# A three-layer forward pass: the opening and the sums of squares of a norm rearranged

## The chip, the cores and the metric

One core of a Trainium2 chip runs the whole program. The metric is the device time of one execution in microseconds; the kernel before takes 2764.75 us, the median of three runs (2763.87 to 2766.82).

## What is computed

Three transformer-like blocks follow one another on a sequence of 512 tokens of width 1024 (528 with 16 extra tokens in the first block). Each begins with an RMS norm and a wide projection, goes through its own mixing (attention of several kinds, a recurrence, a gated memory), and ends with an output projection, a residual addition, another norm and a gated feed-forward part whose result is added to the residual. What matters here is the norm and the projection behind it:

```python
def _rmsnorm(a, gain):
    af = a.astype(jnp.float32)
    af = af * lax.rsqrt(jnp.mean(af * af, axis=-1, keepdims=True) + EPS)
    return (af * gain.astype(jnp.float32)).astype(a.dtype)
...
    z = u @ w_up
```

Everything is in float32.

## The kernel before

**Layout and units.** The residual stream `h` lies transposed: 8 tiles (chunks) of 128 features by the tokens. A weight unit is 1024 inputs by 128 outputs, 8 chunks of 128x128, and is loaded by SyncE's queue (SP) with one transfer of 512 KB into a ring of four buffers (`load_unit`, L355). To keep float32 accuracy, each operand is split into a high part in the fp32r format and a low part, the rest. A chunk of a unit is three matmuls: high weights with high inputs, high weights with low inputs, low weights with high inputs. ScalarE makes the high weights (`hi`, L363), VectorE the low ones (`lo`, L369), two units ahead of TensorE. The same is done to the inputs: `Inputs` (L665 high on ScalarE, L673 and L675 low on VectorE), or `Normed` (products L710, high L695, low L700), which multiplies by the root first.

**Lines.** A `Line` is a matrix product of n units, a unit per output tile (L594). `Added` is the line that adds each finished tile to the residual (L847, L849 on VectorE); `Glu` is the feed-forward's first half (gates scaled on GpSimd, L904; Silu on ScalarE, L891). `down` is the feed-forward's second half, three `Added` lines in a row of 8, 8 and 6 chunks.

**Order.** Every stage gives each engine's program as a generator that yields a planned time, counted in units, ahead of its instructions; `weave` merges the generators of all stages by these times into one fixed queue per engine. The time only sets the order: an instruction whose wait isn't fulfilled holds up all that stands behind it on its engine. A `Line` yields its chunk k of unit u at `at + u + k/8` on TensorE, its high weights at the end of a unit on ScalarE.

**The sums (`Sums`, L717).** While an `Added` line runs, its finished tiles are squared on ScalarE (L741), the squares of tiles 0 to 6 are added up on GpSimd (L756, six additions into `acc`), and TensorE sums over the features with matmuls by a matrix of ones (L766): first `acc`, planned 0.3 units ahead of the end of the line, then the square of the last tile, planned 0.4 units behind it. ScalarE loads the table set that holds Ln and Exp (L295) right ahead of the last square, and makes the root with Ln (L747) and Exp (L748). There are seven such sums. After three of them (near 628, 1006 and 1463 us) the next line starts from the raw tiles, and the root is multiplied in behind its matmuls. After the two that run side by side near 1845 us (`one` and `two`; `SecondRoot` makes the root of `two` at L797 and L798), and after that near 2376 us, the next line's inputs are products with the root. The last one (2749 us) stands ahead of the output (`Final`, L823).

**The opening.** `Prepare` (L2082 on) loads small constants and parameters on SP, the input in four transfers on ScalarE's queue (L2139), squares it (L2149) and sums the squares on TensorE (L2167). `NormedInput` then loads the table set, makes the root (L405, L407), has the first two weight units split, and makes products (L435), high parts (L414) and low parts (L428) chunk by chunk. The first line, `Halved` (L1991), cuts the 528 tokens in two halves of 264 and does all chunks of the first half, then all of the second (L2028).

Of the kernel before, what the change touches and what calls it, by code (L numbers as in the profile page):

```python
# [239 lines left out]
class Core:  # L240
# [151 lines left out]
class NormedInput:  # L392
# [8 lines left out]
    def high(self, act, first=None):  # L401

        core, T = self.core, self.T
        core.exp_ln(act)
# [12 lines left out]
    def low(self, dve, first=None):  # L417
# [3 lines left out]
        def part(k):  # L421
# [295 lines left out]
class Sums(Stage):  # L717


    def __init__(self, core, at, d, tiles, ready, T, bank, tmp, r, names, gains=None, first=None):  # L720
        self.core, self.at, self.d, self.tiles, self.ready, self.T, self.bank, self.r = core, at, d, tiles, ready, T, bank, r
        self.gains, self.first = gains, first
        self.sq, self.acc = core.area(tmp, 2, T), core.area(tmp + 2 * T, T)
        self.squared, self.added, self.summed, self.root = (core.take(n, k) for n, k in zip(names, (NC, NC - 2, 1, 1)))
# [7 lines left out]
    def scalar(self, act):  # L732
        core = self.core
        for k in range(NC):
            yield self.at + (k + 1) * self.d + 0.25
            if k == NC - 1 and self.first is None:
                core.exp_ln(act)
# [5 lines left out]
        yield self.end() + 0.55  # L743
# [6 lines left out]
    def pool(self, pool):  # L750
        for k in range(1, NC - 1):
# [6 lines left out]
    def tensor(self, pe):  # L758
        for n, a in enumerate((self.acc, self.sq[:, (NC - 1) % 2])):
            yield self.end() + (-0.3, 0.4)[n]  # L760
            if n == 0:
                pe.wait_ge(self.added.sem, self.added.at(NC - 2))
            else:
                pe.wait_ge(self.squared.sem, self.squared.at(NC))
            for e, (o, w) in enumerate(halves(self.T)):
                last = pe.matmul(self.core.ps[:, self.bank + e, 0:w], self.core.c("ones"), a[:, o:o + w], start=(n == 0), stop=(n == 1))  # L766
# [1224 lines left out]
class Halved(Stage):  # L1991
# [20 lines left out]
    def tensor(self, pe):  # L2012
        core = self.core
        for u in range(self.n):
            s = self.first + u
            wh, wl = core.wh[:, s % 2], core.wl[:, s % 2]
            for e, (o, m) in enumerate(self.cols):
                for k in range(NC):
                    yield self.at + u + (8 * e + k) / 16
                    if k == 0:  # L2020
                        if self.free.at(2 * u + e - 1) > 0:
                            pe.wait_ge(self.free.sem, self.free.at(2 * u + e - 1))
                        if e == 0:
                            pe.wait_ge(core.split_done, s + 1)
                    if self.x and u == 0 and e == 0:
                        self.x.ready(pe)(k)
                    for n, (w, x) in enumerate(((wh, core.xh), (wh, core.xl), (wl, core.xh))):
                        last = pe.matmul(self.place(e), w[:, k, :], x[:, k, o:o + m], start=(k == 0 and n == 0),  # L2028
                                         stop=(k == NC - 1 and n == 2))
                last.then_inc(core.used if e else self.half.sem, 1)  # L2030

    def scalar(self, act):
# [6 lines left out]
        if self.x:  # L2039
            self.x.high(act, first)  # L2040
# [13 lines left out]
    def vector(self, dve):  # L2054
# [36 lines left out]
class Prepare(Stage):  # L2091
# [17 lines left out]

    def sync(self, sp):  # L2110
# [3 lines left out]
        sp.dma_start(core.par[:, 0:NC], d["params"][:, 0:NC]).then_inc(self.small.sem, 16)  # L2114
        yield -0.5
# [19 lines left out]
    def scalar(self, act):  # L2135
        core, T = self.core, self.T
        yield -20
        for i in range(4):
# [1534 lines left out]
```

## Time and profile before

| | |
|---|---|
| median of three runs | 2764.75 us |
| the profiled execution | 2761.72 us |
| its span | 2759.9 us |
| mean granted clock of TensorE | 0.972 |
| TensorE matmuls busy | 2617.1 us |
| VectorE, ScalarE, GpSimd busy | 1517.5, 1039.5, 331.8 us |

The span is the time from the first to the last recorded instruction; the execution's own time has 1.8 us more around it. TensorE (PE) is the busiest engine by far. Its records overlap, since matmuls are pipelined: the distance between two starts is the cost of one, not the length of a record. The granted clock is 1.00 at 2.4 GHz and 0.50 at 1.2 GHz.

### The profile page before, as it was taken

How to read it: one execution, taken by the hardware profiler on the slowest of the kernel's cores; microseconds unless marked ns; L12 is line 12 of the kernel's file. 1: busy time of each engine (PE TensorE's matmuls, PEld its weight loads, DVE VectorE, ACT ScalarE, POOL GpSimd, SP SyncE). 2: the span in 40 equal slices, each digit the busy share in tenths (PEclk: the TensorE clock that was granted, in tenths of full speed). 3: DMA queues.
4: the chain of work that ended last, by engine and by line, in shares of the span. 5: the costliest groups of instructions: out<-in, count | busy, mean ns of one | idle time of the engine just before them, and what ended most of it. 6: DMA issues, size and time to landing. Idle time of an engine off the chain costs nothing.

```text
span 2759.9 us, 35657 instructions
## 1 busy us (share of the span) xinstructions
PE 2617.1 (95%) x14330; PEld 2117.2 (77%) x14330; DVE 1517.5 (55%) x2528; ACT 1039.5 (38%) x1824; POOL 331.8 (12%) x270
## 2 busy tenths in 40 slices
PE   7989999999999999999889999999999999899998
PEld 6778788898998866866657777867766677688886
DVE  3787654455445456477746778454743544433444
ACT  3366454433223252234443223255332433322323
POOL 0043310012222010010012222020000000100001
PEclk8999999999999999998899999999989999999999
DMA  3211112222232331320024664232211122233332
GB/s 124 72 47 55 54 56 67 64 91 84 92 93 91 99 130 46 121 70 1 1 69 146 200 201 154 93 106 84 84 58 50 47 91 86 83 94 97 92 99 69
DMA packets 70850, 239.01 MB, mean 87 GB/s; under 512 B 12212, under 2 KB 13109, under 8 KB 70430
## 3 DMA queue, kind: packets, MB, share of 16 engines
q1 hardware_dynamic: 63054, 208.88, 24.2%
q10 hardware_dynamic: 7632, 27.86, 3.0%
q8 instruction: 114, 1.87, 0.3%
q14 instruction: 50, 0.41, 0.0%
HBM read 234.06 MB, written 2.64 MB: 86 GB/s over the span
## 4 chain that ended last, share of the span: by engine, by line
PE 63%; DVE 10%; ACT 4%; issue 2%; POOL 1%; ACTq 0%; DVEq 0%; POOLq 0%
PE ps L594 53%; DVE wl L369 2%; PE ps L2733 2%; ACT wh L363 1%; PE ps L3410 1%; DVE xl L675 1%; PE ps L1798 1%; PE ps L1782 1%; DVE arena L1061 1%; PE ps L1809 1%; DVE arena L3089 1%; PE ps L3396 1%; PE ps L1647 1%; PE ps L766 1%; DVE xl L673 0%
## 5 line engine op out<-in xcount | busy, mean ns | idle before, releaser
L594 PE MATMUL ps<-xh,wh 128*128 128x512 f32 (+1 forms) x2728 | 1013.6, 386 | 25.4 <-DVE xl L675 7.4
L594 PE MATMUL ps<-xl,wh 128*128 128x512 f32 (+1 forms) x2728 | 993.2, 378 | 0.0
L594 PE MATMUL ps<-xh,wl 128*128 128x512 f32 (+1 forms) x2728 | 989.0, 377 | 0.0
L369 DVE TENSOR_TENSOR wl<-ring,wh 128x1024 fp32r<-128x1024 f32 x374 | 471.5, 1261 | 623.2 <-ACT wh L363 622.6
L363 ACT ACTIVATE wh<-ring 128x1024 fp32r<-128x1024 f32 x374 | 395.2, 1057 | 953.7 <-PE ps L594 851.9
L594 PEld LDWEIGHTS ps<-xh,wh 128*128 128x128 f32 x2728 | 503.1, 190 | 157.6 <-issue 45.0
L594 PEld LDWEIGHTS ps<-xh,wl 128*128 128x128 f32 x2728 | 502.3, 190 | 98.3
L594 PEld LDWEIGHTS ps<-xl,wh 128*128 128x128 f32 x2728 | 501.2, 190 | 98.4 <-issue 6.5
L2028 PE MATMUL ps<-xh,wh 128*128 128x264 f32 (+1 forms) x816 | 259.6, 318 | 9.6 <-DVE xl L428 9.6
L756 POOL TENSOR_TENSOR arena<-arena 128x512 f32<-128x512 f32 (+1 forms) x42 | 71.5, 1708 | 1368.6 <-ACT arena L741 1368.6
L2028 PE MATMUL ps<-xl,wh 128*128 128x264 f32 (+1 forms) x816 | 234.3, 287 | 0.0
L2028 PE MATMUL ps<-xh,wl 128*128 128x264 f32 (+1 forms) x816 | 234.2, 287 | 0.0
L2028 PEld LDWEIGHTS ps<-xh,wh 128*128 128x128 f32 x816 | 156.9, 192 | 37.9 <-issue 20.4
L2028 PEld LDWEIGHTS ps<-xl,wh 128*128 128x128 f32 x816 | 157.7, 193 | 1.0
L2028 PEld LDWEIGHTS ps<-xh,wl 128*128 128x128 f32 x816 | 157.2, 193 | 0.0
L847 DVE TENSOR_TENSOR h<-ps,h 128x512 f32<-128x512 f32 (+1 forms) x64 | 44.3, 691 | 151.2 <-PE ps L594 151.2
L904 POOL TENSOR_TENSOR arena<-arena 128x516 f32<-128x516 f32 (+1 forms) x44 | 81.0, 1840 | 220.1 <-ACT arena L883 220.1
L891 ACT ACTIVATE arena<-arena 128x512 f32<-128x512 f32 x44 | 27.8, 632 | 202.8 <-DVE arena L923 202.8
L849 DVE SCALAR_TENSOR_TENSOR h<-ps,mod,h 128x512 f32<-128x512 f32 x40 | 30.0, 751 | 111.6 <-PE ps L594 111.6
L907 POOL TENSOR_TENSOR arena<-arena 128x512 f32<-128x512 f32 x44 | 58.4, 1327 | 159.3 <-ACT arena L891 159.3
L675 DVE TENSOR_TENSOR xl<-arena,xh 128x512 fp32r<-128x512 f32 (+1 forms) x108 | 72.3, 728 | 7.4 <-ACT xh L665 7.3
L1061 DVE CUSTOM_DVE_ANT_0 arena<-arena 128x1024 f32<-128x1024 f32 x48 | 69.8, 1488 | 0.0
(391 smaller groups left out, 2711.9 us busy)
## 6 DMA issues: line engine op xcount, KB each, us to landing
ring<-in_weights SPq DMA_DIRECT2D x374, 512.0 KB, 3.5
arena<-in_w_ada ACTq DMA_DIRECT2D x48, 512.0 KB, 4.5
arena<-in_cmp_w SPq DMA_DIRECT2D x2, 2048.0 KB
h<-in_x ACTq DMA_DIRECT2D x4, 528.0 KB, 6.2
arena<-strip_scratch SPq DMA_DIRECT2D x8, 264.0 KB, 3.7
out_features<-arena SPq DMA_DIRECT2D x8, 256.0 KB, 2.1
con<-in_consts SPq DMA_DIRECT2D x1, 777.0 KB, 10.9
arena<-in_c ACTq DMA_DIRECT2D x1, 512.0 KB, 3.8
```

The source lines that it names most:

```text
L363: act.activation(flat(self.wh[:, s % 2]), flat(self.ring[:, s % RING]), ACT.Copy).then_inc(self.hi_ready, 1)
L369: dve.tensor_tensor(flat(self.wl[:, s % 2]), flat(self.ring[:, s % RING]), flat(self.wh[:, s % 2]).bitcast(F32), ALU.subtract).then_inc(se ...
L594: last = pe.matmul(self.place(u, e), w[:, k, :], x[:, k, o:o + m], start=(k == 0 and i == 0), stop=(k == self.chunks - 1 and i == 2))
L675: ins = dve.tensor_tensor(xl, a, xh, ALU.subtract)
L756: pool.tensor_tensor(self.acc, self.sq[:, 0] if k == 1 else self.acc, self.sq[:, k % 2], ALU.add).then_inc(self.added.sem, 1)
L847: ins = dve.tensor_tensor(out, self.got(u), out, ALU.add)
L849: ins = dve.scalar_tensor_tensor(out=out, in0=self.got(u), scalar=self.scale[u], in1=out, op0=ALU.mult, op1=ALU.add)
L904: pool.tensor_tensor(g, g, self.r_gate, ALU.mult).then_inc(self.gate_scaled.sem, 1)
L907: pool.tensor_tensor(self.mid[:, j, 2], self.mid[:, j, 2], self.r, ALU.mult).then_inc(self.scaled.sem, 1)
L1061: dve.tensor_tensor_reduce(out=w, in0=w, in1=self.spread, scale=1.0, scalar=0.0, op0=ALU.mult, op1=ALU.add, accum_out=self.parts[:, (n + e ...
L2028: last = pe.matmul(self.place(e), w[:, k, :], x[:, k, o:o + m], start=(k == 0 and n == 0), stop=(k == NC - 1 and n == 2))
L2733: last = pe.matmul(core.ps[:, self.place(n) + e, 0:c], w[:, k, :], x[:, k, o:o + c], start=(k == lo and i == 0), stop=(k == hi - 1 and i = ...
```

## The change

1. In the opening, SP issues two of the four input loads, ahead of the weights, and ScalarE the other two. The table load of `NormedInput.high` is taken out, so that the one that `Prepare` issues at the start serves. The two first weight units are split ahead of the root, with the high part made by a copy on VectorE (`first_hi`). The first unit of the first line goes chunk by chunk through both halves.
2. In all sums, GpSimd adds the squares of tiles 0 to 5 only, and TensorE takes three addends: `acc`, the square of tile 6 and that of tile 7. The table load is planned 0.4 units ahead of the end of the line.
3. Three sums (near 628, 1006 and 1463 us) get `late=True`: all three addends stand 0.65 units into the next line, behind its chunk 5, and Ln and Exp at 0.85.

```diff
+    def first_hi(self, dve, s):
+        dve.wait_ge(self.arrived[s], 16)
+        flat = lambda a: a.rearrange("p c n -> p (c n)")
+        dve.tensor_copy(flat(self.wh[:, s]), flat(self.ring[:, s])).then_inc(self.hi_ready, 1)
...
-    def high(self, act, first=None):
+    def high(self, act):
         core, T = self.core, self.T
-        core.exp_ln(act)
...
-        if first:
-            first(act)
-        else:
-            core.split_first(act, core.split_hi)
...
+        first(dve)
         dve.wait_ge(self.root.sem, self.root.at(1))
...
-            if k == 1:
-                if first:
-                    first(dve)
-                else:
-                    core.split_first(dve, core.split_lo)
...
     def scalar(self, act):
         core = self.core
         for k in range(NC):
+            if k == NC - 1 and self.first is None:
+                yield self.end() - 0.4
+                core.exp_ln(act)
             yield self.at + (k + 1) * self.d + 0.25
-            if k == NC - 1 and self.first is None:
-                core.exp_ln(act)
...
-        yield self.end() + 0.55
+        yield self.end() + (0.85 if self.late else 0.55)
...
-        for k in range(1, NC - 1):
+        for k in range(1, NC - 2):
             yield self.at + (k + 1) * self.d + 0.4
...
-        for n, a in enumerate((self.acc, self.sq[:, (NC - 1) % 2])):
-            yield self.end() + (-0.3, 0.4)[n]
+        for n, a in enumerate((self.acc, self.sq[:, (NC - 2) % 2], self.sq[:, (NC - 1) % 2])):
+            yield self.end() + (0.65 if self.late else (-0.5, 0.05, 0.4)[n])
             if n == 0:
-                pe.wait_ge(self.added.sem, self.added.at(NC - 2))
+                pe.wait_ge(self.added.sem, self.added.at(NC - 3))
             else:
-                pe.wait_ge(self.squared.sem, self.squared.at(NC))
+                pe.wait_ge(self.squared.sem, self.squared.at(NC - 2 + n))
...
-            for e, (o, m) in enumerate(self.cols):
-                for k in range(NC):
-                    yield self.at + u + (8 * e + k) / 16
+            halves_first = [(e, k) for e in range(2) for k in range(NC)]
+            chunks_first = [(e, k) for k in range(NC) for e in range(2)]
+            for i, (e, k) in enumerate(chunks_first if self.x and u == 0 else halves_first):
+                o, m = self.cols[e]
+                yield self.at + u + i / 16
...
             for s in range(self.begin, self.first + 2):
+                if self.x:
+                    core.first_hi(dve, s)
                 core.lo(dve, s)
...
+    def load(self, eng, i):
+        two = slice(2 * i, 2 * i + 2)
+        eng.dma_start(self.core.h[:, two], self.core.dram["x"].rearrange("p (c t) -> p c t", c=NC)[:, two]).then_inc(self.x[i].sem, 16)
...
         sp.dma_start(core.par[:, 0:NC], d["params"][:, 0:NC]).then_inc(self.small.sem, 16)
+        for i in (1, 3):
+            self.load(sp, i)
         yield -0.5
...
-        for i in range(4):
-            act.dma_start(core.h[:, 2 * i:2 * i + 2], self.core.dram["x"].rearrange("p (c t) -> p c t", c=NC)[:, 2 * i:2 * i + 2]).then_inc(
-                self.x[i].sem, 16)
+        for i in (0, 2):
+            self.load(act, i)
         core.exp_ln(act)
```

## Rows read from the trace of the kernel before

**Rows 1.** The page, part 1: busy time, share and instructions of each engine.

```profile
PE 2617.1 (95%) x14330; PEld 2117.2 (77%) x14330; DVE 1517.5 (55%) x2528; ACT 1039.5 (38%) x1824; POOL 331.8 (12%) x270
```

**Rows 2.** Waits of TensorE, whole span: us in total, times, longest.

```profile
PE ps L766 <- ACT arena L741: 14.1, 7, 3.2
...
PE ps L766 <- POOL arena L756: 3.8, 2, 3.0
```

**Rows 3.** Timeline, 0 to 42 us: start, us, what, [idle before <- releaser].

```profile
5.51 1.18 ACT L2149 ACTIVATE arena<-h 128x528 f32<-128x528 f32 x2 [1.17 <-DMA par<-in_params]
...
6.29 9.48 PE L2167 MATMUL ps<-arena,con 128*128 128x264 f32 x32 [6.29 <-ACT arena L2149]
...
15.81 1.28 ACT L295 ACT_TABLE_LOAD   x1 [1.25 <-PE ps L2167]
17.10 0.70 ACT L405 ACTIVATE arena<-ps,con 128x528 f32<-128x528 f32 x1
...
18.59 1.45 DVE L435 SCALAR_TENSOR_TENSOR arena<-h,par,arena 128x528 f32<-128x528 f32 x2 [17.73 <-ACT arena L407]
19.96 2.35 DVE L369 TENSOR_TENSOR wl<-ring,wh 128x1024 fp32r<-128x1024 f32 x2
...
22.23 0.70 DVE L428 TENSOR_TENSOR xl<-arena,xh 128x528 fp32r<-128x528 f32 x1
...
23.77 0.64 ACT L414 ACTIVATE xh<-arena 128x528 fp32r<-128x528 f32 x1 [2.33 <-DVE arena L435]
...
30.76 1.50 DVE L428 TENSOR_TENSOR xl<-arena,xh 128x528 fp32r<-128x528 f32 x2
...
39.60 0.28 PE L2028 MATMUL ps<-xh,wl 128*128 128x264 f32 x1
```

**Rows 4.** Windows of the opening: busy per engine, granted clock, DMA share, GB/s.

```profile
7.00:8.00 1.00, 1.00 (x4) 0.80 (x3) 0.00 (x0) 0.00 (x0) 0.00 (x0) 1.00 1.01 412
...
34.00:36.00 2.00, 2.00 (x11) 2.00 (x10) 0.17 (x2) 0.00 (x0) 0.00 (x0) 0.50 0.00 0
...
37.00:38.00 1.00, 1.00 (x9) 1.00 (x8) 0.00 (x0) 0.00 (x0) 0.00 (x0) 0.89 0.00 0
```

**Rows 5.** Timeline near 1006 us, TensorE and VectorE.

```profile
1003.12 0.40 PE L594 MATMUL ps<-xl,wh 128*128 128x512 f32 x1
1003.35 0.40 PE L594 MATMUL ps<-xh,wl 128*128 128x512 f32 x1
...
1004.84 3.08 DVE L673 SCALAR_TENSOR_TENSOR xl<-h,par,xh 128x512 fp32r<-128x512 f32 x3
...
1006.76 2.08 PE L766 MATMUL ps<-arena,con 128*128 128x512 f32 x2 [3.01 <-POOL arena L756]
...
1016.43 1.71 PE L766 MATMUL ps<-arena,con 128*128 128x512 f32 x2 [2.83 <-ACT arena L741]
...
1022.05 0.69 DVE L991 TENSOR_TENSOR arena<-ps,arena 128x512 f32<-128x512 f32 x1 [6.63 <-PE ps L594]
```

**Rows 6.** Timeline of TensorE near 628 and 1463 us.

```profile
631.37 1.14 PE L766 MATMUL ps<-arena,con 128*128 128x258 f32 x4 [1.78 <-ACT arena L741]
632.16 0.59 PE L594 MATMUL ps<-xh,wh 128*128 128x258 f32 x2
...
1468.33 1.13 PE L766 MATMUL ps<-arena,con 128*128 128x512 f32 x2 [1.89 <-ACT arena L741]
...
1484.43 0.47 PE L594 MATMUL ps<-xh,wh 128*128 128x512 f32 x1 [1.06 <-DVE wl L369]
```

**Rows 7.** Timeline near 1845 us, TensorE and ScalarE.

```profile
1839.96 2.35 PE L766 MATMUL ps<-arena,con 128*128 128x512 f32 x4 [0.81 <-POOL arena L756]
...
1845.50 1.28 ACT L295 ACT_TABLE_LOAD   x1
```

**Rows 8.** Timeline near 2382 us, TensorE, and near 2747 us, ScalarE.

```profile
2382.39 2.07 PE L766 MATMUL ps<-arena,con 128*128 128x512 f32 x2 [3.17 <-ACT arena L741]
...
2747.41 1.28 ACT L295 ACT_TABLE_LOAD   x1 [4.94 <-PE ps L594]
```

More of the change, by code:

```diff
@@ L415, in high, with low @@
                            bias=self.shifts[k] if self.shifts else 0.0).then_inc(self.hi.sem, 1)
-    def low(self, dve, first=None):
+    def low(self, dve, first):
         core, T, out = self.core, self.T, self.out
@@ L717, with __init__ @@
 class Sums(Stage):
-    def __init__(self, core, at, d, tiles, ready, T, bank, tmp, r, names, gains=None, first=None):
+    def __init__(self, core, at, d, tiles, ready, T, bank, tmp, r, names, gains=None, first=None, late=False):
         self.core, self.at, self.d, self.tiles, self.ready, self.T, self.bank, self.r = core, at, d, tiles, ready, T, bank, r
-        self.gains, self.first = gains, first
+        self.gains, self.first, self.late = gains, first, late
         self.sq, self.acc = core.area(tmp, 2, T), core.area(tmp + 2 * T, T)
-        self.squared, self.added, self.summed, self.root = (core.take(n, k) for n, k in zip(names, (NC, NC - 2, 1, 1)))
+        self.squared, self.added, self.summed, self.root = (core.take(n, k) for n, k in zip(names, (NC, NC - 3, 1, 1)))
     def end(self):
@@ L758, in tensor @@
     def tensor(self, pe):
-        for n, a in enumerate((self.acc, self.sq[:, (NC - 1) % 2])):
-            yield self.end() + (-0.3, 0.4)[n]
+        for n, a in enumerate((self.acc, self.sq[:, (NC - 2) % 2], self.sq[:, (NC - 1) % 2])):
+            yield self.end() + (0.65 if self.late else (-0.5, 0.05, 0.4)[n])
             if n == 0:
-                pe.wait_ge(self.added.sem, self.added.at(NC - 2))
+                pe.wait_ge(self.added.sem, self.added.at(NC - 3))
             else:
-                pe.wait_ge(self.squared.sem, self.squared.at(NC))
+                pe.wait_ge(self.squared.sem, self.squared.at(NC - 2 + n))
             for e, (o, w) in enumerate(halves(self.T)):
-                last = pe.matmul(self.core.ps[:, self.bank + e, 0:w], self.core.c("ones"), a[:, o:o + w], start=(n == 0), stop=(n == 1))
+                last = pe.matmul(self.core.ps[:, self.bank + e, 0:w], self.core.c("ones"), a[:, o:o + w], start=(n == 0), stop=(n == 2))
         last.then_inc(self.summed.sem, 1)
@@ L2016, in tensor @@
             wh, wl = core.wh[:, s % 2], core.wl[:, s % 2]
-            for e, (o, m) in enumerate(self.cols):
-                for k in range(NC):
-                    yield self.at + u + (8 * e + k) / 16
[L2020 to L2030, printed above, removed]
+            halves_first = [(e, k) for e in range(2) for k in range(NC)]
[3 more added lines that the diff above has]
+                yield self.at + u + i / 16
+                if k == 0:
+                    if self.free.at(2 * u + e - 1) > 0:
+                        pe.wait_ge(self.free.sem, self.free.at(2 * u + e - 1))
+                    if e == 0:
+                        pe.wait_ge(core.split_done, s + 1)
+                if self.x and u == 0 and e == 0:
+                    self.x.ready(pe)(k)
+                for n, (w, x) in enumerate(((wh, core.xh), (wh, core.xl), (wl, core.xh))):
+                    last = pe.matmul(self.place(e), w[:, k, :], x[:, k, o:o + m], start=(k == 0 and n == 0),
+                                     stop=(k == NC - 1 and n == 2))
+                if k == NC - 1:
+                    last.then_inc(core.used if e else self.half.sem, 1)
     def scalar(self, act):
@@ L2039, in scalar @@
         if self.x:
-            self.x.high(act, first)
+            self.x.high(act)
         else:
@@ L2924, in mixing_end @@
     stages += [inputs, out]
-    sums = Sums(core, NC, 1, h, out.ready, T, 4, sums_tmp, r, names)
+    sums = Sums(core, NC, 1, h, out.ready, T, 4, sums_tmp, r, names, late=True)
     inputs = Inputs(core, h, 2 * NC - 1, T, gain("ffn_norm"), out.ready)
@@ L2930, in mixing_end @@
     stages += some
-    sums = Sums(core, last.at, last.d, late, last.ready, SEQ, 4, sums_tmp, core.area(28984, SEQ), names)
+    sums = Sums(core, last.at, last.d, late, last.ready, SEQ, 4, sums_tmp, core.area(28984, SEQ), names, late=True)
     inputs = Inputs(core, late, at - 1, SEQ, gain("attn_norm_2"), last.ready)
@@ L3552, in mixing_end_2 @@
     out = Added(core, at, WHOLE, (6, 7, 0, 1), inputs, NC, h)
-    sums = Sums(core, at, 1, h, out.ready, T, 4, tmp, r, names)
+    sums = Sums(core, at, 1, h, out.ready, T, 4, tmp, r, names, late=True)
     stages = [inputs, out, sums]
```

## The prediction

> **What bounds the kernel now.** I read the page first: TensorE is busy for 95% of the span [rows 1], so a change can only pay where TensorE waits or runs at half rate. Then the waits of TensorE [rows 2]: the matmuls that sum the squares (L766) waited 14.1 us for ScalarE's squares and 3.8 us for GpSimd's adds, 17.9 us over seven sums. The timeline of the opening [rows 3] and of each seam [rows 5 to 8] then shows what is late. The reader should see two kinds of seam. Where the next line starts from the raw tiles (near 628, 1006 and 1463 us) the sums only block TensorE's own queue. Where the next stage needs the root itself (near 1845, 2382 and 2749 us) they lie on the path.
>
> The profiled execution took 2761.72 us, of which 2759.9 are its span; the median is 2764.75, 3.0 above it. The sum is made against the profiled execution and carried over to the median unchanged.
>
> **The opening.** Today TensorE's last sum ends at 15.77 (6.29 + 9.48), a table load of 1.28 follows, then Ln and Exp, and VectorE starts at 18.59 [rows 3]. The load goes: -1.3. From there to the end of the first low part (22.23 + 0.70 = 22.93) are 4.34 us, because VectorE makes two products and then the two weight splits (19.96, 2.35) first. After the change the splits are ahead of the root; one product (half of 1.45), one high part (0.64), one low part (0.70) and two hand-overs of some 0.08 remain, 2.2: another -2.1.
>
> The splits get two copies on VectorE. No copy of 128x1024 is in the rows; bounds are the subtraction of that size (half of 2.35) above and 0 below, and I take the upper end, the nearest row. Copies and splits then take at most 4.7 us. Their cover is the sums: VectorE can use the root at 17.3. They start when the weights land. On SP two input loads now pass the weights; all input (four loads of 528 KB, 2.16 MB) and one unit (128x1024 floats, 0.52 MB) at the 412 GB/s of [rows 4] are 6.5 us after the first bytes near 3 us (an estimate of the start of the loads), so unit 0 lands near 9.5 and unit 1 near 10.8, and the splits end near 14. Three microseconds of cover are left; past them each microsecond is paid in full. The constants and parameters behind on SP move by about 1.5 us too, and cost nothing: the first one is used after the last low part. The input's new order I price at 0: the squares start when the small parameters are there (5.51 [rows 3]) and then keep the common pace of ScalarE and TensorE, not that of the loads. Bounds: a gain of 1, a loss of 0.5.
>
> The inputs are now 3.4 us earlier. Low parts come every 1.42 us (22.23 to 30.76 in six steps), so the last one ends near 28.9 instead of 32.26 (30.76 + 1.50). Today the second half of the unit (24 matmuls) is still to do then, at half rate until 37 us [rows 4], and the unit ends at 39.88: 7.6 us. With both halves in every chunk, six matmuls stand behind the last low part, at some 0.2 us each (11 in the 2.00 us of 34 to 36), with the hand-over 1.4: -6.2. Six at half rate also just fit between two low parts. The opening's sum is 9.6. The clock is the doubt: it was granted at 0.50 (1.2 GHz) while there were gaps, and rose at 37, some 5 us after the last one. If that repeats, the second unit runs some 3.5 us at half rate and loses 1.7; if the closer work lifts the clock sooner, nothing is lost. I take 0.8: **8.8**, between 7 and 11.
>
> **One addend more.** The last square but one is now added by TensorE. At 631.37 an addend starts and the next line's matmuls follow at 632.16 [rows 6]: 0.79. Above it stands the pair's whole record, 1.13. I take 0.8 a sum. GpSimd has one add less; it was waited for at 1006 and 1840 only.
>
> **Seams where the sums only block.** There they move behind chunk 5 of the next line's first unit.
> Near 628 a wait of 1.78 goes and 0.8 comes: **1.0**, between 0 and 1.8. The table load, now among the high parts, delays the last ones by 1.28, and the last square by less; five chunks hide that.
> Near 1006 both waits (3.01 and 2.83) and the half rate behind each go [rows 5]. From the last matmul before the first wait (ends 1003.75) to the first addition after the next unit (1022.05) are 18.3 us. After the change there are 30 matmuls of 0.23 and three addends of 0.8 in it, 9.3. I add 1.2 for new waits: tile 7 is added behind the low parts on VectorE, so its square comes near 1012.0, some 0.4 after the first two addends, and chunks 4 and 5 wait a little for their low parts. That leaves 7.8; I take **7.5**, between 4 and 8.5.
> Near 1463 a wait of 1.89 goes and 0.8 comes. But root, Silu table and first high part follow on ScalarE at the time of before, since six chunks and three addends take as long as four chunks, the wait and one addend. The fourth unit's weights then come no earlier, and the wait of 1.06 at 1484.43 [rows 6] becomes 2: **0**, between a loss of 0.5 and a gain of 1.
>
> **Seams where the root is the path.** Near 1845 [rows 7] the 0.81 wait for GpSimd goes and the load of 1.28 leaves the path; the two roots share ScalarE, and the earlier one clears it for the other: **2.5**, between 1.3 and 3. Near 2382 [rows 8] the load goes, and the last addend, now after a pause of 1 us instead of 3.17, should take 1.0 at the full rate instead of 2.07: **2.3**, or 1.0 if the clock stays down. Near 2749 the last square waits for VectorE's addition (some 0.75, as long as a product) instead of the load of 1.28 [rows 8]: **0.5**, between 0.3 and 0.7.
>
> The load is followed at once by the next instruction: 15.81 + 1.28 = 17.09, and Ln starts at 17.10 [rows 3], so a load off the path is worth 1.28. The Trainium skill (ScalarE: Activation LUTs, "What ACT_TABLE_LOAD costs") puts a drain of 1.38 us beside each load; by it four loads off the path give an estimated 5.5 us more. The rows don't show it.
>
> **Sum:** 8.8 + 1.0 + 7.5 + 0 + 2.5 + 2.3 + 0.5 = 22.6. 2761.72 - 22.6 = 2739.1 for the profiled execution, 2764.75 - 22.6 = **2742** for the median. The bounds together give 13 to 28 us.
>
> **Rivals.**
> 1. *New waits take the place.* With the table load among the high parts and low parts at the pace of 1.03 (3.08 for three [rows 5]), the last square comes some 3 us later than I think, and the sums wait for it where they now stand. For it: they still wait for the last square. Against: six chunks (4 us) stand ahead. The seam at 1006 gives 4, 628 gives 0, the others 3, the opening 7: 14 us, 2751. Chance 0.20.
> 2. *More than forecast.* The clock rises early in the opening, two queues start the squares sooner, and 1463 keeps its microsecond: 29 us, 2736. Chance 0.11.
> 3. *A pause that the records hide at each table load*, of the load's own length: 4 x 1.28 = 5.1 more, 2737. Against: the 0.01 us between load and Ln. Chance 0.02. (This is the drain of the Trainium skill's page above.)
> 4. *It doesn't reach the end.* VectorE, the busiest engine beside TensorE in the first block, swallows the opening's gain, and the new addends (7 x 0.8 = 5.6) most of the others': 2761. Against: nothing in the first block starts before the opening's line. Chance 0.05.
> 5. *Slower.* The opening's line now keeps a short gap in every chunk, at 0.50. If the clock stays there beyond that line, each microsecond at half rate costs half of one. It decides once such stretches grow by 2 x (22.6 + 5.5) = 56 us; at 70 us the kernel takes 2777, 12 more than before. Against: gapless work raised it at 37. Chance 0.03.
>
> At 1006 the records show what a pause does: 3.01 us without work, and the pair behind it takes 2.08. The Trainium skill (TensorE: Matmul & The Clock Gate, "HAM oscillation") says of waits between bursts that the next burst starts throttled each time; by that rule, too, the trace agrees.
>
> **Numbers.** The forecast has 0.59; its own range is 2737 to 2748. To hold 8 in 10 the range takes in the first rival: 2735 to 2753. Differences within 0.2% (5.5 us) can't be told from none. Faster 0.91, same 0.06, slower 0.03.
>
> **What would show it.** In the opening: no table load near 15.8, VectorE's copies done before 14, the first low part near 19.4, the first unit done near 30. At 1006: no wait at L766 above 1 us and no half rate. At 1463: the wait for the low weights grows to 2. Near 2382: Ln starts 2 to 2.5 us sooner after the unit's end. L766 has 48 matmuls instead of 32, and its waits are under 4 us together. A first unit that ends after 33, or waits above 8 us at L766, would make the forecast wrong.

## The result, and the profile after

| | before | changed |
|---|---|---|
| median, five runs each | 2766.82 us (2763.87 to 2767.0) | 2742.64 us (2737.73 to 2749.81) |
| ratio to before | | 0.9922, 95% interval 0.9909 to 0.9934 |
| profiled execution | 2761.72 us | 2737.73 us |
| its span | 2759.9 us | 2735.6 us |
| mean granted clock | 0.972 | 0.978 |

By the ratio the changed kernel is faster by 0.78% (21.6 us); the two medians differ by 24.2 us. The forecast was 2742 us. The two profiled spans differ by 24.3 us. Beside [rows 1], part 1 of the page of the changed kernel:

```profile
PE 2610.8 (95%) x14346; PEld 2114.1 (77%) x14346; DVE 1514.5 (55%) x2530; ACT 1036.0 (38%) x1821; POOL 320.1 (12%) x263
```

TensorE has 16 matmuls more (48 for the sums instead of 32), ScalarE three instructions fewer (one is the table load, two are the opening's high splits) and GpSimd seven. The waits of TensorE over the whole span (us in total, times, longest), to be read against [rows 2]; the line of the sums is L765 now:

```profile
PE ps L591 <- DVE wl L375: 8.2, 10, 2.4
...
PE ps L765 <- ACT arena L740: 1.6, 2, 0.9
```

The 17.9 us at the sums are 1.6 us, and none is for GpSimd. The timeline of the changed kernel's opening, beside [rows 3]:

```profile
1.66 1.28 ACT L295 ACT_TABLE_LOAD   x1 [1.66 <-PEq L3674]
...
4.83 1.18 ACT L2158 ACTIVATE arena<-h 128x528 f32<-128x528 f32 x2 [1.89 <-DMA par<-in_params]
...
9.93 0.69 DVE L369 CAST wh<-ring 128x1024 fp32r<-128x1024 f32 x1 [9.06 <-DMA ring<-in_weights]
...
12.52 1.23 DVE L375 TENSOR_TENSOR wl<-ring,wh 128x1024 fp32r<-128x1024 f32 x1
...
15.23 0.70 ACT L410 ACTIVATE arena<-ps,con 128x528 f32<-128x528 f32 x1 [1.29 <-PE ps L2176]
...
16.64 1.45 DVE L437 SCALAR_TENSOR_TENSOR arena<-h,par,arena 128x528 f32<-128x528 f32 x2 [2.89 <-ACT arena L412]
...
18.11 0.71 DVE L429 TENSOR_TENSOR xl<-arena,xh 128x528 fp32r<-128x528 f32 x1
...
26.66 1.50 DVE L429 TENSOR_TENSOR xl<-arena,xh 128x528 fp32r<-128x528 f32 x2
...
29.44 1.06 ACT L363 ACTIVATE wh<-ring 128x1024 fp32r<-128x1024 f32 x1
```

The first weights land at 9.93; copies and splits are done at 13.75, ahead of the root. Ln follows the last sum with no load between. The last row is the high part of the next weight unit, which needs the end of the first unit; the same instruction in the kernel before:

```profile
38.17 1.06 ACT L363 ACTIVATE wh<-ring 128x1024 fp32r<-128x1024 f32 x1 [4.32 <-PE ps L2028]
```

So the opening gave 38.17 - 29.44 = 8.7 us. Near 1006 us, beside [rows 5], TensorE and VectorE of the changed kernel:

```profile
996.24 2.07 DVE L670 SCALAR_TENSOR_TENSOR xl<-h,par,xh 128x512 fp32r<-128x512 f32 x3
...
1000.00 0.50 PE L591 MATMUL ps<-xh,wh 128*128 128x512 f32 x1 [0.58 <-DVE xl L670]
...
1001.48 2.90 PE L765 MATMUL ps<-arena,con 128*128 128x512 f32 x6
1003.82 0.79 PE L591 MATMUL ps<-xh,wh 128*128 128x512 f32 x1
...
1005.88 0.69 DVE L990 TENSOR_TENSOR arena<-ps,arena 128x512 f32<-128x512 f32 x1 [2.22 <-PE ps L591]
```

All six matmuls of the three addends run in one piece, 2.34 us from their start to that of the line's next matmul, 0.78 an addend; one wait of 0.58 stands in place of 3.01 and 2.83. Three low parts in a row take 2.07 us where they took 3.08 [rows 5]. That isn't 1.03 each: taken apart, two of the three took 0.74 and the middle one 1.75. The kernel before:

```profile
1005.50 1.75 DVE L673 SCALAR_TENSOR_TENSOR xl<-h,par,xh 128x512 fp32r<-128x512 f32 x1
```

```profile
1005.17 1.53 POOL L756 TENSOR_TENSOR arena<-arena 128x512 f32<-128x512 f32 x1 [4.83 <-ACT arena L741]
```

GpSimd's addition of a square ended at 1006.70, and the long low part 0.55 us behind it. It is the same near 622.81 and 1459.81 us; in the changed kernel no addition stands beside a low part. Near 628 and 1463 us, beside [rows 6]:

```profile
622.58 2.78 PE L765 MATMUL ps<-arena,con 128*128 128x258 f32 x12
...
1472.35 0.47 PE L591 MATMUL ps<-xh,wh 128*128 128x512 f32 x1 [2.44 <-DVE wl L375]
```

The wait at 628 is gone. At 1463 the wait for the fourth unit's low weights grew from 1.06 to 2.44. Near 1845 and 2382 us, beside [rows 7, 8], TensorE and ScalarE:

```profile
1828.18 1.28 ACT L295 ACT_TABLE_LOAD   x1
...
1831.60 3.98 PE L765 MATMUL ps<-arena,con 128*128 128x512 f32 x8
...
2359.52 1.12 PE L765 MATMUL ps<-arena,con 128*128 128x512 f32 x2 [0.89 <-ACT arena L740]
2360.68 0.69 ACT L746 ACTIVATE arena<-ps,con 128x512 f32<-128x512 f32 x1 [1.22 <-PE ps L765]
```

The load stands 3.4 us ahead of the sums, and the last addend takes 1.12 instead of 2.07.

**Where the 24.3 us are.** I lined up the same instruction in both traces (ScalarE's high weights, one a unit) and read how much sooner it starts in the changed kernel: 8.7 us behind the opening, 7.2 ahead of the seam at 628, 8.6 behind it, 16.2 behind 1006, 11.7 ahead of 1463 and 10.5 behind it, 13.6 behind 1845, 12.1 at 2021, 21.5 at 2053, 23.8 behind 2382. The seams are the forecast's; the rest lies between them, and one piece, 9.4 us from 2021 to 2053, is as large as the opening. There the memory gates of the third block are computed, in code that the change doesn't touch. The window from 2000 to 2060 us (length, busy time of PE, PEld, DVE, ACT and POOL with counts, granted clock, DMA share, GB/s), in the kernel before and in the changed one:

```profile
2000.00:2060.00 60.00, 54.06 (x161) 34.29 (x160) 22.82 (x37) 23.07 (x35) 0.00 (x0) 0.77 0.17 53
```

```profile
2000.00:2060.00 60.00, 56.46 (x210) 38.54 (x211) 22.57 (x36) 21.75 (x32) 0.00 (x0) 0.94 0.20 62
```

At a clock of 0.77, 28 of 60 us are at the half rate (60 x 0.23 x 2); at 0.94 it is 7.

### The profile page after: what moved, and what is told of

The parts are those of the page before. It is cut to its first block, busy times and chain, and to the rows that moved or that the text cites. A ratio compares the mean times of both kernels' runs of the same rounds, so it can differ in the third digit from the quotient of the medians.

```text
span 2735.6 us, 35675 instructions
## 1 busy us (share of the span) xinstructions
PE 2610.8 (95%) x14346; PEld 2114.1 (77%) x14346; DVE 1514.5 (55%) x2530; ACT 1036.0 (38%) x1821; POOL 320.1 (12%) x263
## 3 DMA queue, kind: packets, MB, share of 16 engines
q1 hardware_dynamic: 63342, 209.96, 24.3%
## 4 chain that ended last, share of the span: by engine, by line
PE 64%; DVE 10%; ACT 4%; issue 2%; POOL 0%; ACTq 0%; DVEq 0%
PE ps L591 54%; DVE wl L375 2%; PE ps L2742 2%; ACT wh L363 1%; DVE arena L1060 1%; PE ps L3419 1%; DVE xl L672 1%; PE ps L1797 1%; PE ps L1781 1%; PE ps L1808 1%; DVE arena L3098 1%; PE ps L765 1%; PE ps L3405 1%; PE ps L1646 1%; DVE arena L1837 0%
## 5 line engine op out<-in xcount | busy, mean ns | idle before, releaser
L755 POOL TENSOR_TENSOR arena<-arena 128x512 f32<-128x512 f32 (+1 forms) x35 | 60.2, 1726 | 1343.7 <-ACT arena L740 1343.7
```

The source lines that it names most:

```text
L755: pool.tensor_tensor(self.acc, self.sq[:, 0] if k == 1 else self.acc, self.sq[:, k % 2], ALU.add).then_inc(self.added.sem, 1)
```

## The experiments

I held that the change pays at its own seams, and that the 9.4 us are a matter of the clock. The rivals: the gates' gain belongs to the work that was moved, or it is chance of one execution; and single parts of the change are worth other sums than I gave them. Where a table gives "gain at" a time, it is read in the profiles as above, against the profile of before.

**The changed kernel once more**, without an edit, five executions.

> The changed kernel once more, unaltered, to see what differs between executions of one program. Its five times ranged over 12 us where the kernel before had 3. Theory A (fixed savings): span 2735 to 2748, and wherever it is longer than the first profile, the first line, 1006 and 2382 look the same and the time is lost elsewhere. Theory B (the clock by chance): the memory gates near 2013 us run at half rate for 4 us or for 20 us from one execution to the next, worth up to 9 us, and that is the whole spread.

Measured: 2742.94 us (2740.56 to 2744.44), ratio 0.9921 (0.9908 to 0.9934). The gates' gain is there again (9.4 us). But of the opening's 8.4 us at 52 only 0.7 are left at 175 us. The window from 48 to 68 us of this execution:

```profile
48.00:68.00 20.00, 20.00 (x61) 13.11 (x60) 4.86 (x6) 4.51 (x11) 0.00 (x0) 0.57 0.15 50
```

and of the first profile of the same program:

```profile
48.00:68.00 20.00, 20.00 (x97) 13.61 (x96) 7.86 (x10) 6.60 (x16) 0.00 (x0) 1.00 0.23 64
```

Clock 0.57 in the one, 1.00 in the other; 36 matmuls fewer in the same 20 us. TensorE shows no gap in either. Up to 50.13 us the two timelines are the same within 0.13 us, wait by wait. Small attention matmuls over 32 rows (L2286) stand there between those of the line; one pair takes 1.24 us in this execution

```profile
52.15 1.24 PE L2286 MATMUL ps<-arena 32*128 32x264 f32 x2
```

and 0.71 in the first:

```profile
52.68 0.71 PE L2286 MATMUL ps<-arena 32*128 32x264 f32 x2
```

So one program has executions that differ by a stretch of 17 us at the half rate. Over the timed executions, too, the time goes with the mean clock, though they don't tell which stretch it is (clock, us):

```
changed:      .978 2737.73  .973 2749.81  .977 2742.64  .978 2739.04  .973 2747.35
once more:    .975 2744.44  .975 2743.96  .977 2742.94  .977 2742.84  .976 2740.56
```

**The parts apart.** *Opening only*: the kernel before with part 1 of the change.

```diff
-        core.exp_ln(act)
...
+        first(dve)
         dve.wait_ge(self.root.sem, self.root.at(1))
...
+        for i in (1, 3):
+            self.load(sp, i)
...
-                for k in range(NC):
-                    yield self.at + u + (8 * e + k) / 16
+            for i, (e, k) in enumerate(chunks_first if self.x and u == 0 else halves_first):
```

> Only the opening's edits, all sums as before. Theory A: 8.7 us faster than before, as the two profiles differ at the end of the first unit (38.0 against 29.3), 2756 to 2759. Theory B: the shift alone also moves where half-rate stretches fall, above all at the memory gates, so the gain is anywhere from 4 to 18 us and doesn't equal the 8.7 seen at the first unit.

Measured: 2759.92 us (2752.45 to 2767.86, twelve runs), ratio 0.9983 (0.9971 to 0.9995). *Sums only*: the kernel before with parts 2 and 3.

```diff
-        for n, a in enumerate((self.acc, self.sq[:, (NC - 1) % 2])):
+        for n, a in enumerate((self.acc, self.sq[:, (NC - 2) % 2], self.sq[:, (NC - 1) % 2])):
...
+    sums = Sums(core, NC, 1, h, out.ready, T, 4, sums_tmp, r, names, late=True)
```

> Only the edits of the sums, the opening as before. Theory A: from the two profiles 1.2 near 628, 7.6 near 1006, 0 near 1463, 2 to 3 near 1845, 2.4 near 2382, 0.5 at the end: 14 us, 2751 to 2754. Theory B: 14 at these seams, and up to 9 more or 5 less elsewhere, wherever the clock falls differently.

Measured: 2749.95 us (2747.42 to 2753.92), ratio 0.9949 (0.9937 to 0.9961). By medians (before 2765.65, once more 2742.94) the sums are worth 15.7 us, the opening 5.7, both together 22.7. The opening's 8.7 us are there at 38 us in the profile of the opening alone too (8.9), but the half rate at 52 us (clock 0.57 there as well) takes 7.7 of them (8.6 at 52, 0.9 at 175). Its twelve executions spread over 15 us, clocks 0.967 to 0.974.

**The sums not moved** (*not late*): the changed kernel with its three `late=True` taken out.

```diff
-    sums = Sums(core, at, 1, h, out.ready, T, 4, tmp, r, names, late=True)
+    sums = Sums(core, at, 1, h, out.ready, T, 4, tmp, r, names)
```

> The changed kernel with no sum moved into the next line: all at -0.5, 0.05 and 0.4 units. Forecast theory (the move removes the waits near 628, 1006, 1463): waits come back at L765 there, about 1 us at 628, 2 to 3 at 1006 with half rate behind it, and the time is 4 to 7 us longer than the changed kernel. Rival (the earlier table load and the addends on TensorE had done it): no wait above 0.5 us comes back, and the time is the same within 1 us.

Measured: 2753.62 us (2752.22 to 2758.19), ratio 0.9963 (0.995 to 0.9975); 10.7 us more than the changed kernel once more. At 1006 the seam itself still gives 6.2 of the 7.6 us, since two waits have become one of 2.2. But 4.7 us go again between two high parts behind it (those at 1028.58 and 1040.07 us in the kernel before), at a half rate from 1023 to 1033 us of this run. It begins 13 us after the end of that wait. The windows of this run:

```profile
1016.00:1020.00 4.00, 4.00 (x18) 2.93 (x16) 2.28 (x5) 2.41 (x4) 0.00 (x0) 1.00 0.46 131
1020.00:1024.00 4.00, 3.50 (x10) 1.97 (x10) 2.57 (x5) 2.82 (x4) 0.00 (x0) 0.87 0.10 8
1024.00:1028.00 4.00, 4.00 (x7) 1.31 (x5) 0.30 (x1) 0.69 (x1) 0.00 (x0) 0.50 0.33 123
```

That the wait causes it is not shown. The table load alone (below), with waits of 3.0 and 1.3 us here, loses 4.7 us in the same place; the addends alone, with a longer wait (2.7), lose nothing.

At 1463 the sum that was left in place is better, by 2.4 us: a gain across the seam of 1.2 instead of a loss of 1.2. And the gates are back at a clock of 0.74 from 2000 to 2060 us.

**Table load only** and **addends only**, one execution each, on the kernel before. The first plans the table load 0.4 units ahead of the end of the line:

```diff
+            if k == NC - 1 and self.first is None:
+                yield self.end() - 0.4
+                core.exp_ln(act)
             yield self.at + (k + 1) * self.d + 0.25
```

> The kernel before with the table load 0.4 units ahead of the line's end, and nothing else. Forecast theory: the load leaves the path, so against the kernel before the weights' high parts after the seams come 1.3 us sooner at 1845, 1.3 at 2382 and 0.5 at the end; at 628 and 1463 the wait at L766 shrinks by up to 1.3; at 1006 the second wait (2.83) shrinks by up to 1.3 and the first (for GpSimd) stays. If the load costs more on the path than its record (the drain of the Trainium skill's page), it is 2.7 at 1845 and at 2382. Clock theory: outside the seams the profile differs wherever half-rate stretches fall otherwise.

The second has GpSimd add one square less and TensorE three addends at -0.5, 0.05 and 0.4 units:

```diff
-            yield self.end() + (-0.3, 0.4)[n]
+            yield self.end() + (-0.5, 0.05, 0.4)[n]
```

> The kernel before with three addends on TensorE at -0.5, 0.05 and 0.4 units, the table load still ahead of the last square. Forecast theory: the wait for GpSimd near 1004 (3.01) and near 1840 (0.81) is gone; each sum costs TensorE 0.8 more; near 628 and 1463 the next line's first unit ends where it did, because the addend fills the wait for the last square. Near 1006 the last square is still waited for, near 2 us. Rival (TensorE's extra addend costs more than GpSimd's wait): 628, 1463 and 2382 become 0.8 later each.

Measured: 2755.49 and 2758.45 us, before 2767.99. What each gave across a seam, in us:

| seam | table only | addends only | both, not moved | changed |
|---|---|---|---|---|
| 628 | 1.2 | 0.7 | 1.2 | 1.4 |
| 1006 | 3.1 | 5.7 | 6.2 | 7.6 |
| 1463 | 1.2 | 0.8 | 1.2 | -1.2 |
| 1845 | 1.7 | 2.4 | 2.3 | 3.1 |
| 2382 | 1.4 | 0.9 | 2.4 | 2.4 |

The parts overlap, since they clear the same waits. Near 1006 (1000 to 1030 us) the waits of TensorE with the table load alone:

```profile
PE ps L767 <- POOL arena L757: 3.0, 1, 3.0
...
PE ps L767 <- ACT arena L742: 1.3, 1, 1.3
```

and with the addends alone:

```profile
PE ps L766 <- ACT arena L741: 2.7, 1, 2.7
```

Each clears a part of the two waits of [rows 5]: the load more than half of ScalarE's, the addends all of GpSimd's. Where the root is the path (2382), an early load gives 1.4 us, its own length and hardly more.

**The opening's steps.** *Halves first*: the changed kernel with the first unit in its old order.

```diff
-            for i, (e, k) in enumerate(chunks_first if self.x and u == 0 else halves_first):
+            for i, (e, k) in enumerate(halves_first):
```

> The changed kernel with the first unit in the old order, all chunks of one half and then of the other. From the two profiles: the last low part ends at 28.2 as in the changed kernel, and the first unit ends 24 matmuls later than the first half, 3 us at the full rate or 5.3 at half, so near 31.3 or 33.7 instead of 29.2. My forecast had put 6.2 us on this order; the profile of the changed kernel says 4.6 with the clock's share in it. A third outcome, that the gaps in the first half keep the clock at 0.50 as in the kernel before, gives the 33.7.

*Splits behind*: the first weight units are split behind the root again, the high part on ScalarE.

```diff
         act.activation(self.r, self.r, ACT.Exp, scale=-0.5).then_inc(self.root.sem, 1)
+        first(act)
...
-        first(dve)
         dve.wait_ge(self.root.sem, self.root.at(1))
...
+            if k == 1:
+                first(dve)
```

> The changed kernel with the two first weight units split behind the root again, high parts on ScalarE, as before. Forecast theory: the first low part comes 2.1 us later than in the changed kernel, and so does the end of the first unit (31.3 instead of 29.2). Clock theory: TensorE's pause ahead of the first line grows from 3.8 to 5.9 us, so the line starts at 0.50 and is held back by its own matmuls (1.32 per chunk) only where they take over 1.42; then still 2.1. After 50 us both theories leave the profile open: a half-rate stretch of 17 us at 48 to 68 takes 8 us, or doesn't come.

*Delayed*: three more squares of chunk 0, overwritten by the next, stand ahead in `Prepare.scalar` and delay the whole opening.

```diff
+            if k == 0:
+                for _ in range(3):
+                    core.act.do(act, act.activation(self.sq[:, 0], core.h[:, 0], ACT.Square))
```

> The changed kernel with three more squares of the first chunk ahead of the opening's sums, some 2.2 us that nothing covers. Theory A (each span is the sum of its parts): every high part of the weights comes 2.2 us later than in the changed kernel's profiles, from the first to the last. Theory B (half-rate stretches fall by where the work stands in time): 2.2 later at the first unit, then jumps of several us of either sign at 48 to 68, 1236 to 1420 or 2008 to 2050, with half-rate stretches begun or ended there.

Measured, one execution each: 2744.57, 2742.71 and 2741.2 us. The start of the next unit's high part tells the order's price. With halves first:

```profile
27.00 1.50 DVE L429 TENSOR_TENSOR xl<-arena,xh 128x528 fp32r<-128x528 f32 x2
...
34.30 1.06 ACT L363 ACTIVATE wh<-ring 128x1024 fp32r<-128x1024 f32 x1 [4.21 <-PE ps L2029]
```

5.8 us lie between the end of the last low part (28.50) and that start; in the changed kernel 29.44 - 28.16 = 1.3. The order by chunks is worth 4.5 us. The clock's part is in it: with halves first the mean from 0 to 40 us is 0.83, in the changed kernel 0.96. With the splits behind:

```profile
16.15 0.70 ACT L410 ACTIVATE arena<-ps,con 128x528 f32<-128x528 f32 x1 [1.31 <-PE ps L2176]
...
21.28 0.70 DVE L430 TENSOR_TENSOR xl<-arena,xh 128x528 fp32r<-128x528 f32 x1
```

The first low part comes 5.13 us after Ln's start, 2.88 in the changed kernel: 2.2 for the splits. The delayed kernel starts the same high part at 32.40, 3.0 later (2.2 were expected), and is some 3 us behind the changed kernel from there to 2399 us (23.8 against 20.4), with no jump of the clock between.

**What the gates depend on.** In 14 profiles the window from 2000 to 2060 us has one of a few clocks:

| the sum near 1463 | profiles | clock |
|---|---|---|
| moved behind chunk 5 | changed, once more, sums only, halves first, splits behind, delayed, filled | 0.94 in all seven |
| in its old place | before, opening only, not late, table only, addends only, moved twice | 0.77, 0.74, 0.74, 0.89, 0.77, 0.74 |
| old place, gates filled | gates filled | 0.97 |

*Moved twice*: the changed kernel with the sum near 1463 in its old place (the other two stay late), five executions.

```diff
     out = Added(core, at, WHOLE, (6, 7, 0, 1), inputs, NC, h)
-    sums = Sums(core, at, 1, h, out.ready, T, 4, tmp, r, names, late=True)
+    sums = Sums(core, at, 1, h, out.ready, T, 4, tmp, r, names)
```

> The changed kernel with the sum near 1463 not moved into the next line (those near 628 and 1006 stay moved). Four profiles say that after this seam the moved sum gives nothing or takes 1.2 us (steps of -1.2 in all kernels that move it), while the table load alone gave 1.3 and all three addends unmoved 1.6. Theory: the root is what the fourth unit waits for through Silu and the modulation, so an earlier root helps: 2.4 to 2.8 us sooner than the changed kernel at 1507 in the profile, and 2740 as a median if the clock falls alike. Rival (my forecast: nothing happens there whatever TensorE does): the same within 0.5 us at 1507.

Measured: 2750.28 us (2749.41 to 2758.39), ratio 0.995 (0.9938 to 0.9963). Across 1463 it gains 1.2 and not -1.2, as left in place it should; the wait for the low weights is 1.06. At the gates it loses 1.5 where the changed kernel gains 9.4, and its five executions have clocks of 0.969 to 0.973. The timeline of TensorE ahead of the gates:

```profile
2011.05 0.41 PE L3273 MATMUL ps<-con,arena 4*128 4x4 f32 x4 [2.22 <-DVE arena L3303]
...
2012.69 2.07 PE L3287 MATMUL ps<-arena,con 4*128 4x512 f32 x2
```

and its windows:

```profile
2012.00:2016.00 4.00, 4.00 (x7) 1.65 (x7) 0.21 (x2) 0.60 (x1) 0.00 (x0) 0.50 0.45 131
...
2028.00:2032.00 4.00, 4.00 (x7) 1.33 (x5) 0.00 (x0) 1.56 (x2) 0.00 (x0) 0.50 0.00 0
```

The windows of the changed kernel:

```profile
2012.00:2016.00 4.00, 4.00 (x10) 2.11 (x8) 0.09 (x2) 0.60 (x1) 0.00 (x0) 0.63 0.42 131
2016.00:2020.00 4.00, 4.00 (x11) 1.74 (x11) 0.00 (x0) 0.60 (x1) 0.00 (x0) 0.94 0.00 0
```

The changed kernel has the same wait (2.26) and falls too, but is back at the full rate within 4 us. In the kernel that moves two sums the half rate stays on through matmuls over 4 rows (L3287) set between those of the line. What differs is when the clock falls. The windows from the end of the wait, in the kernel that moves two sums:

```profile
2011.05:2011.73 0.68, 0.68 (x6) 0.62 (x7) 0.68 (x1) 0.68 (x1) 0.00 (x0) 1.00 0.00 0
2011.73:2039.04 27.31, 27.31 (x49) 13.93 (x48) 4.14 (x10) 5.55 (x11) 0.00 (x0) 0.50 0.13 39
```

and in the changed kernel:

```profile
2010.92:2013.03 2.11, 2.10 (x9) 1.10 (x9) 1.17 (x2) 0.71 (x1) 0.00 (x0) 1.00 0.06 8
2013.03:2016.44 3.41, 3.41 (x8) 2.06 (x8) 0.00 (x0) 0.60 (x1) 0.00 (x0) 0.50 0.45 149
```

The clock falls 0.68 us after the wait in the one and 2.11 in the other.

*Gates filled*: the kernel that moves two sums, with two constant matmuls into an unread bank ahead of the gates' wait, six executions.

```diff
         yield at + 0.9
+        for _ in range(2):
+            pe.matmul(core.ps[:, 5, :], core.c("ones"), core.c("causal", 512), start=True, stop=True)
         pe.wait_ge(self.rows.sem, self.rows.at(1))
```

> The kernel of the run before (sum near 1463 not moved) with two matmuls of constants (512 columns, never read, some 1.7 us) in TensorE's wait of 2.22 us ahead of the memory gates. In that kernel the clock was at 0.50 from 2012 to 2039, 27 us of half rate, in every kernel that moves the sum near 1463 for 3 to 7 us only. Theory 1 (that wait lets the clock fall, and the matmuls of 4 rows with their waits behind it keep it down): no half rate from 2012 on, 10 to 12 us less than 2750, so 2738 to 2741, the fastest version. Theory 2 (the gates' own pattern does it, whatever stands ahead): the stretch stays and the time is 2750. Theory 3 (it hangs on something between 1463 and 2000): it stays too, or is cut to part.

Measured: 2740.68 us (2737.89 to 2747.47, six runs), ratio 0.989 (0.9857 to 0.9924). Its timeline and window:

```profile
2013.58 1.88 PE L3272 MATMUL ps<-con 128*128 128x512 f32 x4
2016.01 0.41 PE L3275 MATMUL ps<-con,arena 4*128 4x4 f32 x4 [0.54 <-DVE arena L3305]
```

```profile
2020.00:2024.00 4.00, 4.00 (x12) 1.90 (x13) 0.00 (x0) 0.92 (x2) 0.00 (x0) 1.00 0.02 6
```

The wait of 2.22 is 0.54, the clock stays at 1.00, and the step across the gates is a gain of 10.9 us instead of a loss of 1.5. The two intervals (0.9857 to 0.9924, 0.9938 to 0.9963) don't meet. So in this kernel the wait ahead of the gates is what sets off the half rate, and work in it prevents it; how long the half rate lasts once it is there is another question (see **Open** below). This kernel has the best median and ratio of all, though its interval reaches into that of the changed kernel (0.9909 to 0.9934); that it beats it is not shown. *Filled*: the changed kernel with two constant matmuls of 264 columns into an unread bank ahead of the first wait of the 32-row matmuls, five executions; `self.shared.open`, which stood behind that wait, is moved ahead of them.

```diff
+            self.drained[n] = self.shared.open(pe)
             if n == 0:
+                for _ in range(2):
+                    pe.matmul(core.ps[:, 5, 0:264], core.c("ones"), core.c("causal", 264), start=True, stop=True)
                 pe.wait_ge(self.copied.sem, self.copied.at(1))
-            self.drained[n] = self.shared.open(pe)
```

> The changed kernel with two matmuls of constants (264 columns, never read) in TensorE's wait for GpSimd's copies at 46.7 us, which is 0.71 us long; they take 0.88, so 0.2 too much. If that pause is what lets the clock fall at 51 us for 17 us in some executions, the stretch is gone from all of them and the median is 4 to 8 us below the changed kernel's, 2735 to 2739. If it is the small matmuls of 32 rows behind it (L2286), nothing changes: 2743, and the stretch at 48 to 68 is there or not as before.

Measured: 2742.39 us (2738.31 to 2744.33), ratio 0.9914 (0.99 to 0.9927). Its profile has no half rate from 48 to 68 us, but neither have nine others of 14, and its executions have clocks of 0.975 to 0.978 like those of the changed kernel. Whether the filling prevents that stretch stays open. All four profiles that have it (once more, opening only, not late, gates filled) are of kernels with the new opening as it stands, of which there are six profiles; the four with the old opening and the four with an altered one have none. Whether the new opening makes the stretch likelier is not shown by so few.

## Why the prediction was right, step by step

| part | forecast | measured in the two profiles |
|---|---|---|
| opening | 8.8 | 8.7 |
| 628 | 1.0 | 1.4 |
| 1006 | 7.5 | 7.6 |
| 1463 | 0 | -1.2 |
| 1845 | 2.5 | 3.1 |
| 2382 | 2.3 | 2.4 |
| 2749 | 0.5 | 0.5 |
| between the seams | 0 | 1.9 |
| sum (of unrounded rows) | 22.6 | 24.3 |

**The opening** came out right in total by luck: errors that cancelled. The load was worth its 1.28 us, and the splits 2.16 against 2.1: from VectorE's first product to the end of the first low part 4.34 us became 2.18. The step that failed is "the unit ends at 39.88: 7.6 us". I took the last matmul of [rows 3] for the end of the first unit, and it belongs to the second. The record that shows a unit's end is the high part that waits for it, at 38.17: 5.9 us behind the last low part, not 7.6. With 1.3 left after the change the order by chunks gave 4.6, not 6.2, and the run with halves first gives 4.5. Two other errors made up for it. The 0.8 us that I set aside for the clock weren't needed: from 0 to 40 us the granted clock was 0.79 before and 0.96 after, some 17 and 3 us at the half rate. And the squares started 0.68 us sooner (4.83 against 5.51), which I had priced at 0; the small parameters landed sooner. The copies took 0.69 us each; I had taken the subtraction's 1.2 as upper end, and copies and splits ended at 13.75, near my 14, since the weights landed at 9.93 and not at 9.5. The Trainium skill (VectorE: DVE Perf Modes, "The perf-mode tier table") lists a float32 copy at twice the rate of an operation on two tensors; by it I would have had an estimated 0.6, and the trace agrees (0.69 against 1.23).

**Seams where the sums block.** The working held near 1006 (7.5 against 7.6), and so did 0.8 an addend (0.78). The run without the move shows what the move is for there: 1.4 us at the seam. The 4.7 us that its profile loses behind the seam are not shown to be the move's doing. Near 1463 the direction was right and the size too small. The wait for the fourth unit's weights grew to 2.44 and not to 2: the root and ScalarE's chain behind it come later, and the moved sum costs 2.4 us against the one left in place, in both kernels that leave it (not late and moved twice). Behind the wait of 2.44 TensorE is at the half rate from 1473.7 to 1477.1 us, which those two kernels aren't. So the longer wait (2.44 - 1.06 = 1.4) is not the whole of the 2.4, and how the rest divides is not shown.

**Seams where the root is the path.** 2382 and 2749 came as worked out. 1845 gave 3.1, 0.1 above my upper bound; the parts alone gave 1.7 and 2.4 there.

**Between the seams** I had nothing, and the runs show the largest single piece of the whole: 9.4 us at the gates. Against it stand 7 us of losses in four stretches (175 to 205, 1071 to 1094, 1233 to 1423, 1936 to 1944 us). The largest, 3.3 us, lies where the mean clock from 1200 to 1480 us is 0.87 and was 0.90, some 17 us more at the half rate. That net 1.9 is small is luck of these two executions: the first profile of the changed kernel escaped the half rate at 52 us, which costs 7.7 us in the second.

**The rivals.** New waits (1) did not come: 0.58 us at 1006 and 1.6 in all at the sums. Its "pace of 1.03" for a low part was a mean over one of 1.75 and two of 0.74. That the gain doesn't reach the end (4) is true of a part of the opening's in some executions: 5.7 us by the medians of the opening alone, where 8.9 are there at 38 us; in its profile the half rate at 50 us takes them, not VectorE. The hidden pause at a table load (3) doesn't show: the load alone gives 1.4 us at 2382, where 2.6 would have been due. The mechanism of rival 5 is real but short: the clock does stay at half beyond a pause while work runs without a gap, for 17 us from 50 us on in four of the 14 profiles; "gapless work raised it at 37" was no protection there. Of the signs that I named, all came: no load near 15.8, copies before 14, the first low part at 18.82, the unit's end near 29.4, Ln near 2382 2.3 us sooner after its unit.

**Open.** Why the place of a sum near 1463 decides over the clock at the gates 550 us later. Both kernels have the same wait there, and table load alone, which doesn't move it, is halfway between (0.89). The runs show that the link holds in the profiles and that filling the wait makes it irrelevant. The traces show one thing more: what goes with the place of that sum is when the clock steps against the work. In the seven profiles of kernels that move it the clock falls 2.05 to 2.11 us after the gates' wait ends and stays down for 3.4 us. In the six with the sum in its old place it falls earlier, 0.66 to 1.58 us after, and stays down for 10 to 27 us (0.66 to 0.69: 27; 0.77: 24; 1.24: 10; 1.58: 24, so the distance alone doesn't set the length). The wait of 3.7 us that stands 9.6 us ahead of it has the same order: 1.45 to 1.51 us against 0.07 to 0.98. At 50 us it looks alike. In the four profiles with the stretch the clock had last risen 24.6 to 24.7 us before the first 32-row matmul, in the two of the same opening without it 24.4 and 23.3. What carries the clock's steps along with the work, and what keeps it down, these runs don't show. Not tried was the changed kernel with both fillings, or gates filled with all three sums moved.

## What to carry to other kernels

Find a unit's end by the instruction of another engine that waits for it, not by the last row that looks like it. Where a sum or another late addend blocks a queue whose next work doesn't need it, move it behind as much of that work as its own chain leaves room for, and follow the chain (root, table, next weights) before moving: near 1463 the move cost 2.4 us. And read the granted clock by stretches in more than one execution before a gain of under 10 us is put down to an edit; the wait of 2 us ahead of small matmuls was worth ten here, and constant matmuls in it are a cheap test.

## What the hardware showed that I had not expected

- One program, two executions: the same timeline to 50.13 us within 0.13, then 17 us at the half rate in one and none in the other, which costs the one 7.7 us.
- A wait of 2.22 us ahead of matmuls over 4 rows was followed by some 27 us at the half rate, in which TensorE shows no gap; with the wait filled to 0.54 there were none. In the changed kernel a wait of 2.26 at the same place was followed by 3.4, and the clock fell 2.11 us after it instead of 0.68. The Trainium skill (TensorE: Matmul & The Clock Gate, "HAM oscillation") puts the half rate down to waits between bursts; the gates agree with that as far as the start goes, but there and at 52 us the half rate went on through work without gaps.
- A low part of VectorE (128x512) takes 0.74 us. Beside a GpSimd addition one took 1.75 to 1.80, and ended 0.55 us after the addition, in all three such places of the kernel before; another that began ahead of the addition was not longer (0.74 to 0.75).
- A 128x1024 copy from float32 to fp32r takes VectorE 0.69 us, the subtraction of that size 1.23.
